# Dilated attention on one core: where, and in what shape, the attention output is transposed back

## The reference

```python
s = jnp.einsum('bnqche,bnkche->bnchqk', qs, kw).astype(jnp.float32) * scale + bias
s = jnp.where(mask, s, MASK_VALUE)
m = jnp.max(s, axis=-1, keepdims=True)
e = jnp.exp(s - m)
l = jnp.sum(e, axis=-1, keepdims=True)
o = jnp.einsum('bnchqk,bnkche->bnqche', e.astype(v.dtype), vw)
```

## Time and profile before

| | us |
|---|---|
| median of 3 runs | 2932.22 (2930.03 to 2933.57) |
| the profiled execution, its own time | 2932.87 |
| its span in the trace | 2931.0 |
| TensorE (PE) busy in the span | 2731.9 (93%) |
| VectorE busy | 2045.2 (70%) |
| ScalarE busy | 1559.6 (53%) |
| GpSimd busy | 1053.4 (36%) |

### The profile page before, as it was taken

The page is one execution under the profiler, slowest core; times in us unless marked ns, Lnnn a source line. Parts: engine busy times, 40 slices in busy tenths (PEclk is TensorE's granted clock), DMA queues, the critical chain, the costliest instruction groups (busy, mean ns, idle before and its releaser), DMA issues. The chain is left out here.

```text
span 2931.0 us, 54522 instructions
## 1 busy us (share of the span) xinstructions
PE 2731.9 (93%) x21026; PEld 2233.1 (76%) x21026; DVE 2045.2 (70%) x3027; ACT 1559.6 (53%) x3111; POOL 1053.4 (36%) x803
## 2 busy tenths in 40 slices
PE   7899989999699999989998899899899999799998
PEld 5678867888588888878887678688677788577776
DVE  5767687666799999967777765433567767466675
ACT  6574446644588888867776221322433343455553
POOL 4677656776122222129550543200021111221211
PEclk9999999999899999999999899899999999899999
DMA  3433323332412121023443666242165465744441
GB/s 115 129 108 94 94 80 93 108 108 87 133 24 54 32 53 25 24 63 114 119 119 109 235 217 252 85 145 79 51 181 132 98 158 161 177 148 135 144 155 67
DMA packets 317438, 330.11 MB, mean 113 GB/s; under 512 B 24401, under 2 KB 259969, under 8 KB 314113
## 3 DMA queue, kind: packets, MB, share of 16 engines
q1 hardware_dynamic: 287184, 292.59, 32.8%
q0 software_dynamic: 6912, 23.07, 2.7%
q10 hardware_dynamic: 23088, 11.02, 1.6%
HBM read 217.13 MB, written 109.47 MB: 111 GB/s over the span
## 5 line engine op out<-in xcount | busy, mean ns | idle before, releaser
L1049 PE MATMUL p_acc<-p_y_hi,p_x_hi 128*128 128x512 f32 x904 | 362.2, 401 | 11.4 <-DVE p_y_lo L841 3.8
L1049 PE MATMUL p_acc<-p_y_lo,p_x_hi 128*128 128x512 f32 x904 | 356.4, 394 | 0.0
L1049 PE MATMUL p_acc<-p_y_hi,p_x_lo 128*128 128x512 f32 x904 | 356.1, 394 | 0.0
L562 POOL TENSOR_TENSOR p_x_lo<-k_carry,p_x_hi 128x1024 fp32r<-128x1024 f32 x113 | 281.1, 2494 | 131.9 <-ACT p_x_hi L634 131.9
L1894 ACT ACTIVATE d_e<-d_e,d_neg_top 128x2048 f32<-128x2048 f32 x128 | 256.9, 2007 | 18.9 <-DVE d_neg_top L1974 18.9
L2061 PEld LDWEIGHTS d_out<-d_v,d_w_t 64*128 64x128 f32 x4096 | 248.0, 188 | 11.9 <-ACT d_a_parts L1909 0.8
L920 DVE RECIPROCAL p_aux<-p_aux 128x512 f32<-128x512 f32 x64 | 215.1, 3361 | 57.5 <-ACT p_aux L730 57.5
L2061 PE MATMUL d_out<-d_v,d_w_t 64*128 64x128 f32 x4096 | 249.7, 272 | 0.7 <-ACT d_a_parts L1909 0.7
L1565 PE MATMUL s_acc<-s_y_hi,s_x_hi 128*128 128x512 f32 x560 | 224.1, 400 | 22.0 <-DVE s_x_lo L1369 12.9
L1565 PE MATMUL s_acc<-s_y_lo,s_x_hi 128*128 128x512 f32 x560 | 221.5, 395 | 0.0
L1565 PE MATMUL s_acc<-s_y_hi,s_x_lo 128*128 128x512 f32 x560 | 221.1, 395 | 0.0
(11 more groups left out here) (367 smaller groups left out, 7097.6 us busy)
## 6 DMA issues: line engine op xcount, KB each, us to landing
k_carry<-in_w_in SPq DMA_DIRECT2D x128, 256.0 KB, 3.3
k_carry<-in_a_w_in POOLq DMA_DIRECT2D x72, 256.0 KB, 3.6
cols<-p_z SPq DMA_DIRECT2D x64, 256.0 KB, 2.6
w_q<-q SPq DMA_DIRECT2D x15, 1024.0 KB, 8.2
o_parts<-l_stage SPq DMA_DIRECT2D x192, 66.0 KB, 1.8
m_o<-o_parts SPq DMA_DIRECT2D x48, 264.0 KB, 5.9
k_carry<-cols SPq DMA_DIRECT2D x48, 256.0 KB, 4.7
j_x_second<-x SPq DMA_DIRECT2D x20, 512.0 KB, 3.8
```

The lines of the kernel that those rows point to most:

```text
L562: pool.tensor_tensor(x_lo[:, m % RING], inputs.place(x_place(m)), x_hi[:, m % RING].bitcast(F32), ALU.subtract).then_inc(x_lo_made, 1)
L1049: mm = pe.matmul(bank_of(n, j), x_part[:, n % RING, j, kt], y_part[:, y_slot(n), kt], start=(kt == 0 and m == 0 and not (g == 0 and n % 2 ...
```

## The change

Three things are changed, all in `dilated_attention`:

- `turn_out` makes four transposes of 64x64 in place of two of 128x128: for each unit one per half of the rows, that is per head. The half h is written to `out[:, h, 256:384]`, so to both output banks, beside the columns 0 to 255 of bank 0 which `values` writes and `copy_out` reads. `stage_out` reads the two banks in one copy of the same size.
- turn_out is issued three steps late in place of two and directly behind `transposes(n)`, ahead of `scores(n+2)`. stage_out likewise comes behind `move(n, 1)`, ahead of `top(n+2)`.
- As values and turn_out now share a bank, waits are added: turn_out(n) waits for the copy_out of the step after its own, and values(n) waits for stage_out(n-2).

```diff
             def stage_out(n):
                 dve.wait_ge(o_turned, n + 1)
-                dve.tensor_copy(stage[:, 2 * n % SLOTS:2 * n % SLOTS + 2, 0:2 * HD],
-                                out[:, 1, 0:2 * P].rearrange("p (u n) -> p u n", n=P)).then_inc(staged, 1)
+                dve.tensor_copy(stage[:, 2 * n % SLOTS:2 * n % SLOTS + 2, 0:2 * HD].rearrange("p u (h n) -> p u h n", n=HD),
+                                out[:, :, 2 * P:3 * P].rearrange("p h (u n) -> p u h n", n=HD)).then_inc(staged, 1)
...
-            for n in range(TOTAL + 2):
+            for n in range(TOTAL + 3):
                 if n < TOTAL:
                     move(n, 1)
+                if n >= 3:
+                    stage_out(n - 3)
                 if n + 2 < TOTAL:
                     top(n + 2)
-                if n >= 2:
-                    stage_out(n - 2)
                 if 1 <= n < TOTAL + 1:
                     copy_out(n - 1)
...
             def values(n):
                 wait_moved(pe, n)
                 if n >= 1:
                     pe.wait_ge(o_copied, n)
+                if n >= 2:
+                    pe.wait_ge(staged, n - 1)
...
             def turn_out(n):
-                pe.wait_ge(o_copied, n + 1)
+                pe.wait_ge(o_copied, min(n + 2, TOTAL))
                 if n >= 1:
                     pe.wait_ge(staged, n)
                 for j in range(2):
-                    mm = pe.transpose(out[:, 1, unit_of(j)], o_t[:, n % 2, j], ident[:, :])
+                    for h in range(2):
+                        own = slice(h * HD, (h + 1) * HD)
+                        mm = pe.transpose(out[:, h, 2 * P + j * HD:2 * P + (j + 1) * HD], o_t[own, n % 2, j], ident[own, own])
                 mm.then_inc(o_turned, 1)
...
-            for n in range(TOTAL + 2):
+            for n in range(TOTAL + 3):
                 if n < TOTAL:
                     transposes(n)
+                if n >= 3:
+                    turn_out(n - 3)
                 if n + 2 < TOTAL:
                     scores(n + 2)
-                if n >= 2:
-                    turn_out(n - 2)
                 if 1 <= n < TOTAL + 1:
                     values(n - 1)
```

## The result

| kernel | median us | runs | ratio to the kernel before | 95% interval |
|---|---|---|---|---|
| before | 2931.2 | 12 | 1 | |
| changed | 2939.87 | 12 | 1.0028 | 1.002 to 1.0035 |
| changed, measured again | 2938.74 | 11 | 1.0022 | 1.0013 to 1.0031 |

The changed kernel is slower, by 8.2 us in the first comparison (0.0028 x 2931) and by 6.4 us in the second. The forecast was 2936.5 us, 4.3 us slower, with 2928 to 2945 as its range. The measured time lies in the range and on the side that was forecast; the size is half as large again to twice as large. Both differences are above the 5.9 us that the prediction took as the least that can be told, and it had given slower only 0.38 and no difference that can be told 0.52.

What follows compares the result with a forecast made beforehand. TensorE's stream bounds the kernel before; the change closes a loop through VectorE's copy_out. Periods +2.5 us and the stage's end +1.8 us make +4.3 us on the median of 2932.22: 2936.5 us, range 2928 to 2945 us.

Steps and rivals of the forecast that it cites:

- What bounds before: Dilated stage: TensorE's instruction stream sets the step, with periods of 3.27 us wide and 2.57 us narrow.
- What the change takes out and adds: TensorE's stream per step: 0.37 us of turn_out out, 0.125 us for four transposes in, 0.245 us shorter.
- The loop: Scores, top, copy_out, turn_out, scores across TensorE and VectorE: periods 3.21 us wide, 2.67 narrow, 3.08 mixed; +2.5 us.
- The rest of a step at nothing: move, stage_out, ScalarE's last copy and stores cost nothing; the added wait for staged is free, with 0.42 us to spare.
- The end: Behind the last top, values waits for stage_out in rounds of 2.04 us: 8.8 us instead of 7.00, so +1.8 us.
- B: Rival: the copy is there in time and TensorE's stream stays the bound, 3.02 us periods, 2911.7 us; chance 0.08.
- C: Rival: TensorE's restart after turn_out's wait costs 0.085 us per step, 7.7 us more, 2944.2 us; chance 0.17.
- D: Rival: a term of the loop is shorter by 0.07 us, 6.4 us off, 2930.1 us; chance 0.12.
- The busy-time reading of the copies: VectorE's 2.73 us per wide step is under 3.02, so by busy time copies would not bind, giving 2911.7 us.

Runs made afterwards that it cites:

- The spare copy in the kernel before: Kernel before, plus one VectorE copy of 128 elements per partition ahead of copy_out into a tile nothing reads: 2930.25 us, ratio 1.0001.
- turn_out inside the scores: Changed kernel with turn_out issued between the four bias matmuls and twelve query-key matmuls of scores(n+2): 2920.92 us, ratio 0.9964 to the kernel before.
- the pair of spare copies: The same extra VectorE copy ahead of copy_out in both kernels: changed kernel 2957.84 us, ratio 1.0083; kernel before 2930.25 us, ratio 1.0001.
- The shifted code: Changed kernel with 64 idle transposes ahead of scores(0), moving the place of TensorE's later instructions: 2940.34 us, one run.
- the second profile: Profile from measuring the changed kernel again as it stands: 2938.74 us, ratio 1.0022 to the kernel before.
- shorter rounds: Last five steps keep turn_out's old shape and bank: in the changed kernel 2938.07 us; with turn_out also inside the scores 2916.35 us.

## Why the prediction was right, and what of it was not

- **What bounds before: right.** TensorE's stream set the step. The spare copy in the kernel before left its 91 periods alone to 0.01 us. The list of TensorE's gaps left out the 0.17 us ahead of the transposes, which are there before and after and change nothing in the sum.
- **What the change takes out and adds: right where TensorE is the bound.** values follows the last score pass by 0.33 us (1341.16 to 1341.49; forecast 0.32). Four transposes: forecast 0.125, measured 0.12 without a wait, 0.15 behind the wait and 0.19 inside the scores. TensorE's own stream, forecast at 3.02 us, is 3.07 with turn_out inside the scores; in the changed place my estimate from the rows is 3.21 - 0.17 - 0.03 = 3.01.
- **The loop: right**, shown by the pair of spare copies and by the move into the scores. Forecast periods 3.21, 2.67 and 3.08; measured 3.21, 2.68 and 3.12. In the wide step the longer start of the scores (0.15) was offset, by luck, by a copy and a score term that I had 0.01 us too long each. The 91 periods grew by 4.1 us, not 2.5: 60 x 3.214 + 12 x 3.12 + 19 x 2.685 = 281.3, and the one break of 0.6. The shifted code, without a break, has 281.20: the loop by itself makes 3.4 us.
- **The rest of a step at nothing: right in the middle.** stage_out over two banks takes 0.41, and values waits for none there.
- **The end: the mechanism right, the size off.** +1.8 us was forecast, +2.85 and +3.1 measured. Each round took 2.13 us in place of 2.04, since values starts 0.15 us (1603.92 to 1604.07) behind the stage_out that it waits for, where I took the 0.06 seen for turn_out; the last turn_out, which waits for stage_out, starts 0.15 behind it too (1606.55 to 1606.70). That is 4 x 0.09 us: the forecast's 8.87 and the 9.21 of the profile whose clock stayed at 1.00. The rest, 0.6 and 0.9 us, is the clock: it fell to 1.2 GHz before the last round. I had costed the end at the clock of the rows before.
- **The first four steps**, which I left out of the sum, are 0.7 us shorter than in the profile of the kernel before (11.0 us against 11.73). They take 11.0 us in all other profiles, the spare copy in the kernel before among them: the odd one is the profile before, with its clock of 0.57, and the change has no part in it.
- **The rivals.** B (3.02 us periods) is excluded by the periods; what it describes came true once turn_out stood inside the scores. C, a price of restarting, is there in small: some 0.03 us per step (0.15 behind the wait, 0.12 in the two steps that did not wait), not 0.085. Its verdict (slower by more than 0.2%) holds, mostly through the end. D is excluded.
- **The busy-time reading of the copies.** VectorE stood still for 0.4 to 0.8 us ahead of each top, and yet one copy on it set the period. The section PSUM Bottleneck of the Trainium skill's "TensorEngine Tiling (Array Packing)" had the right suspect, the copy out of PSUM; the trace adds that here it binds by order and latency, and before it binds by load.

The sum of what was measured in the stage is 4.1 + 2.85 - 0.7 = 6.2 us; the change's own part is the 7.0 without the first steps, and 4.2 + 3.1, some 7.2, in the second profile. The forecast had 2.5 + 1.8 = 4.3. What it lacked is 0.9 us in the loop's terms, 0.6 to 0.7 for the break, 0.4 in the rounds of the end and 0.6 to 0.9 for the clock. All these misses go the same way, so the total was not saved by luck; it stayed in the range because the range was wide enough. Between the 7.0 to 7.2 us and the 8.2 of the first comparison there stays some 1 us, less than the half-width of its interval (5.9 to 10.3 us); whether further breaks in slower executions make it was not shown.

## What to carry to other kernels

When a step is moved ahead of another on the busiest engine, look at what it waits for, not at how long it takes: follow the wanted result back until it comes to the engine again, and add up that loop. Moved by 0.55 us within the same stream, the same four instructions went from a wait in nearly every step to a wait in three of them (the end of the stage apart). To find out whether an operation on a half-idle engine is on such a loop, lengthen it by a known amount and see whether the period grows by just that.

## What was not expected of the hardware

- turn_out starts 0.06 us behind the copy_out that it waits for, but 0.15 us behind the stage_out that it waits for in the last round; values starts 0.15 us behind stage_out too. So the delay does not go by the number of semaphores waited for; what sets it was not shown.
- At the end of the stage, with TensorE busy for 2.20 of 4 us, the granted clock fell from 1.00 to 0.5 within the stage in both profiles of the changed kernel. With the same rounds and shifted code it stayed at 1.00 until the stage was nearly over, and with shorter rounds the stage was through before it fell.
- The granted clock fell back to 0.57 for 4 us near the start of the stage in one profile of ten, that of the kernel before, and these steps took 0.7 us longer there than in the other nine.
- TensorE's stream can break off for 0.5 to 0.7 us in the middle of a group of matmuls that wait for nothing.
